# Two more slabs in the first wide stage of a four-branch decoder trunk, and its weights in 1 MB loads from one queue

## The chip, the cores and the metric

The kernel runs on one core of a Trainium2 chip. The metric is the device time in microseconds (us) of one execution; before the change it is 983.06 us, the median of three runs.

## The reference, cut to what matters

Two layers work on x, 256 tokens of 2048 numbers, all in float32. Each layer computes

```
c_act = silu(c)
shift, scl, gate_res = split(c_act @ ada_w[l] + ada_b[l], 3)   # 2048 x 6144 weights, one row of input
h = rms(x) * (1 + scl) + shift
z = h @ w_in[l]                      # layer 0: u_a, q, k, v, g = 48 slabs of 128 columns
y = [pool_mixer or attention ...]    # layer 0: pooling mixer of u_a beside attention of q, k, v
x = x + gate_res * ((y * silu(g)) @ w_out[l])                  # 16 slabs
```

So h of layer 0, which every product of that layer needs, waits for 32 MB of `ada_w`, and those weights serve one single row of input: they cost transfer time and VectorE time, but almost no TensorE time.

## The kernel before

**Weights as slabs.** `w_slabs` holds 141 slabs of 128 columns, 1 MB each, in the order of use: layer 0 has U (0 to 7), q (8 to 15), k (16 to 23), v (24 to 31), g (32 to 47) and its output product (48 to 63); layer 1 begins at 64. From slab 12 on, a slab is split into an upper and a lower part, `whi` (ScalarE, L496) and `wlo` (VectorE, L1204), and h likewise into `hhi` and `hlo`; TensorE makes three products of the fast kind for each of the 16 chunks of h (L835 to L837, for k and v L980 to L983). A slab goes through the buffer `raw` (four halves of 512 KB), loaded two slabs ahead (`AHEAD`).

**The first wide stage.** Slabs 0 to 11 are done differently. TensorE multiplies them unsplit (L893, `unsplit_chunk`): for each chunk c of h in turn it adds the chunk's product to all 12 outputs at once, which stand in six PSUM banks. So it can begin with chunk 0 when a quarter of the `ada_w` sums is there. The weights of this stage are stored chunk by chunk, and a half slab of `raw` is used up after 8 products. The trace has two records for one unsplit product and one for each fast one.

**Units and pieces.** `ada_w` comes as 192 units of 512 KB, 16 to a piece (1024 columns). Pieces 0 to 3 are layer 0's shift and scale: piece p gives chunks 4p to 4p+3 of h. VectorE multiplies each unit by its element of `c_act` and adds it to `acc` (L1214); the units of pieces 2 and 3 are done in two instructions each (L1231, L1234), so that the first half of a piece is ready after 8 units. TensorE sums `acc` over the partitions (L927, `reduce_piece` and `reduce_half`), VectorE keeps the result and normalizes x (L1238, L1251, L1287), and ScalarE adds the shift (L514). The first 64 units use eight slots: four in `ada`, two in `V`, two in `Y`; later ones use the four in `ada`. `UNIT_RATES` says how many units belong to the step of a slab; the units of pieces 4 to 11 are spread over all later stages.

**Order.** All orders are written out by hand, engine by engine, and tied by semaphores. SyncE (SP) issues the units and the slabs from 10 on; ScalarE issues slabs 0 to 9 between its own instructions, and waits there for TensorE to free the halves. SP's queue waits where its next transfer waits. On TensorE `keep_warm` puts small products without use ahead of some chunks (L822).

**Places further on that the change touches.** GpSimd clears `acc` for piece p+2 when piece p is summed (`clear`, L391), and in its program the slopes that the attention adds to the scores of heads 2 to 7 (`slopes`, L399) stand behind `clear(7)`, which waits for the sum of piece 5:

```
            slopes(0, range(0, 2))
            clear(7)
            slopes(0, range(2, HC))
```

Head i of layer 0 is scored on TensorE (L1005, L1006) at the end of step 27+i, and VectorE adds the slopes in the same step (L1387), takes the maxima, and divides (L1415) in the next; TensorE transposes the result (L1017). The weights of the pooling mixer, `PW`, are loaded into `V` by GpSimd (L432) before the first `pool_product` (L955), and `pool_branch` on VectorE makes its input. Where layer 1 begins, VectorE ends layer 0 with `add_x(63)` (L1343), and then makes the new h chunk by chunk with `lo` and `units` written between (L1599 to L1619); layer 1's wide stage (L874, 8 slabs, split) takes half slab c of slabs 64 to 71 for chunk c.

## Time and profile before

| | |
|---|---|
| runs, us | 979.67, 984.81, 983.06 |
| median | 983.06 us |
| span of the profiled execution | 977.3 us |
| device time of the profiled execution | not listed apart from the three runs; the lowest is 979.67 us |
| TensorE busy (PE) | 942.7 us, 96% of the span |
| VectorE busy (DVE) | 822.4 us, 84% |
| ScalarE busy (ACT) | 422.5 us, 43% |
| GpSimd busy (POOL) | 63.5 us, 6% |
| mean granted TensorE clock | 0.991 |
| HBM read over the span | 256.07 MB |

The span runs from the first instruction to the last. Matmuls are pipelined, so that a busy TensorE is not one at its peak: what counts is the distance from one matmul's start to the next. The granted clock is a share of 2.4 GHz; at 0.50 it is the lower level, 1.2 GHz.

### The profile page before, as it was taken

The page shows a single profiled execution, that of the slowest core. Times are in us where ns is not written, and L with a number is a line of the kernel's source. Part 1 is how long each engine was busy: PE and PEld are TensorE (multiplying, and loading weights), DVE is VectorE, ACT ScalarE, POOL GpSimd, SP SyncE. Part 2 cuts the span into 40 slices and gives each one's busy share as a digit, 9 for nine tenths or more (in the row PEclk, how much of TensorE's full clock was granted, in tenths as well). Part 3 has the DMA queues.
Part 4 walks back from the last instruction along what each step waited for, and adds up shares of the span by engine and source line. Part 5 has one row for each costly group of instructions (what it writes and reads, how often), then busy time and mean ns, then how long its engine had stood idle before and what let it go on. Part 6 is the DMA issues. An engine that isn't in the chain of part 4 may idle for free.

```text
span 977.3 us, 18750 instructions
## 1 busy us (share of the span) xinstructions
PE 942.7 (96%) x7042; PEld 908.3 (93%) x7042; DVE 822.4 (84%) x1256; ACT 422.5 (43%) x726; POOL 63.5 (6%) x76
## 2 busy tenths in 40 slices
PE   2999999999999999999999999999999999999998
PEld 2887889999998999999999999999999989998887
DVE  5887968887999778999887999888999986879964
ACT  2220125444655444444444444444556655743331
POOL 1000000010110000132100000000011100000000
PEclk9999998999999999999999999999999999999999
DMA  9999988888876878899959555544455445587962
GB/s 366 409 399 399 379 298 319 293 329 330 325 286 233 294 260 312 322 370 377 339 176 321 193 176 189 175 151 140 164 175 193 172 163 203 199 315 288 360 227 75
DMA packets 77666, 261.26 MB, mean 267 GB/s; under 512 B 7952, under 2 KB 8592, under 8 KB 77344
## 3 DMA queue, kind: packets, MB, share of 16 engines
q1 hardware_dynamic: 72384, 240.90, 67.5%
q10 hardware_dynamic: 2880, 10.49, 2.7%
q0 software_dynamic: 2336, 8.98, 2.6%
q8 instruction: 43, 0.70, 0.3%
q14 instruction: 23, 0.19, 0.1%
HBM read 256.07 MB, written 4.19 MB: 266 GB/s over the span
## 4 chain that ended last, share of the span: by engine, by line
PE 72%; DVE 19%; DMA 4%; issue 2%; ACT 2%; SPq 1%; DVEq 0%; ACTq 0%
PE bank L835 13%; PE bank L836 13%; PE bank L837 13%; PE bank L856 6%; DVE wlo L1204 5%; PE bank L893 4%; PE bank L980 4%; DVE acc L1214 4%; PE bank L983 4%; PE bank L982 4%; PE bank L854 3%; DMA Y<-ada_units 3%; DVE Y L1431 2%; PE bank L927 2%; DVE acc L1234 1%
## 5 line engine op out<-in xcount | busy, mean ns | idle before, releaser
L496 ACT ACTIVATE whi<-raw 128x1024 fp32r<-128x1024 f32 x256 | 270.1, 1060 | 382.3 <-PE bank L837 217.0
L1204 DVE TENSOR_TENSOR wlo<-raw,whi 128x1024 fp32r<-128x1024 f32 x256 | 312.0, 1234 | 74.9 <-ACT whi L496 73.6
L835 PE MATMUL bank<-hhi,whi 128*128 128x256 f32 x912 | 263.8, 289 | 2.5 <-ACT T L741 0.9
L836 PE MATMUL bank<-hlo,whi 128*128 128x256 f32 x912 | 259.3, 284 | 0.0
L837 PE MATMUL bank<-hhi,wlo 128*128 128x256 f32 x912 | 259.1, 284 | 0.0
L1214 DVE SCALAR_TENSOR_TENSOR acc<-ada,cact,acc 128x1024 f32<-128x1024 f32 x144 | 187.4, 1302 | 23.9 <-DMA ada<-ada_units 12.6
L835 PEld LDWEIGHTS bank<-hhi,whi 128*128 128x128 f32 x912 | 176.2, 193 | 5.3 <-issue 3.1
L836 PEld LDWEIGHTS bank<-hlo,whi 128*128 128x128 f32 x912 | 176.2, 193 | 0.1
L837 PEld LDWEIGHTS bank<-hhi,wlo 128*128 128x128 f32 x912 | 176.1, 193 | 0.0
L980 PE MATMUL bank<-whi,hhi 128*128 128x256 f32 x512 | 146.7, 287 | 0.0
L982 PE MATMUL bank<-whi,hlo 128*128 128x256 f32 x512 | 144.9, 283 | 0.0
L983 PE MATMUL bank<-wlo,hhi 128*128 128x256 f32 x512 | 144.9, 283 | 0.0
L980 PEld LDWEIGHTS bank<-whi,hhi 128*128 128x128 f32 x512 | 98.2, 192 | 0.8 <-issue 0.7
L1431 DVE SCALAR_TENSOR_TENSOR Y<-U,par,Y 128x256 f32<-128x256 f32 x240 | 98.6, 481 | 0.0
L982 PEld LDWEIGHTS bank<-whi,hlo 128*128 128x128 f32 x512 | 98.3, 192 | 0.1
L983 PEld LDWEIGHTS bank<-wlo,hhi 128*128 128x128 f32 x512 | 98.2, 192 | 0.0
L856 PE MATMUL bank<-both_g,whi 128*128 128x512 f32 x256 | 89.9, 399 | 0.0
L893 PE MATMUL bank<-X,raw 128*128 128x256 f32 x384 | 86.5, 387 | 1.6 <-DMA raw<-w_slabs 1.5
L893 PEld LDWEIGHTS bank<-X,raw 128*128 128x128 f32 x384 | 74.2, 195 | 12.2 <-issue 1.8
L835 PE MATMUL bank<-both_g,whi 128*128 128x256 f32 x256 | 73.1, 286 | 0.0
L836 PE MATMUL bank<-both_g,whi 128*128 128x256 f32 x256 | 72.5, 283 | 0.0
L837 PE MATMUL bank<-both_g,wlo 128*128 128x256 f32 x256 | 72.4, 283 | 0.0
(195 smaller groups left out, 1220.2 us busy)
## 6 DMA issues: line engine op xcount, KB each, us to landing
raw<-w_slabs SPq DMA_DIRECT2D x260, 512.0 KB, 4.5
ada<-ada_units SPq DMA_DIRECT2D x160, 512.0 KB, 6.6
raw<-w_slabs ACTq DMA_DIRECT2D x20, 512.0 KB, 7.0
V<-ada_units SPq DMA_DIRECT2D x16, 512.0 KB, 9.7
Y<-ada_units SPq DMA_DIRECT2D x16, 512.0 KB, 11.3
X<-xT SPq DMA_DIRECT2D x1, 2048.0 KB, 12.6
x_dram<-X POOLq DMA_DIRECT2D x4, 512.0 KB, 8.5
outT<-X POOLq DMA_DIRECT2D x3, 512.0 KB, 4.9
```

The source lines that it names most:

```text
L496: act.activation(whi[:, slot], raw[:, slot], ACT.Copy).then_inc(hi_done, 1)
L835: mm(out, whi[:, s, k, :], ahi[:, c, :], start=(c == 0), stop=False)
L836: mm(out, whi[:, s, k, :], alo[:, c, :], start=False, stop=False)
L837: last = mm(out, wlo[:, s, k, :], ahi[:, c, :], start=False, stop=(c == KC - 1))
L856: last = mm(out[:], whi[:, s, k, :], flat(both_g[:, c]), start=(c == 0), stop=(c == KC - 1), skip_group_check=True)
L893: last = mm(wide(s), raw[:, slot, k, :], X[:, c, :], start=(c == 0 and s % 2 == 0), stop=(c == KC - 1), skip_group_check=True)
L980: mm(out, hhi[:, c, tokens], upper, start=(c == 0 and q == 0), stop=False, skip_group_check=True)
L982: mm(out, hlo[:, c, tokens], upper, start=False, stop=False, skip_group_check=True)
L983: last = mm(out, hhi[:, c, tokens], lower, start=False, stop=(c == KC - 1), skip_group_check=True)
L1204: dve.tensor_tensor(wlo[:, s], source, whi[:, s].bitcast(F32), ALU.subtract)\
L1214: dve.scalar_tensor_tensor(acc[:, p % 2, :], unit_at(first + u), cact[:, bass.ds(k, 1)], acc[:, p % 2, :], ALU.mult, ALU.add).then_inc(ada ...
L1431: ins = dve.scalar_tensor_tensor(Y[:, j, :], U[:, j, k:k + SEQ], par[:, wcol:wcol + 1], Y[:, j, :], ALU.mult, ALU.add)
```

## The change

- `WIDE[0]` is 14: slabs 12 and 13 join the unsplit stage, in a seventh bank (`M`), and the split slabs begin with 14.
- The 14 slabs are loaded as 14 transfers of 1 MB (`load_wide`), all by SP, into four homes: the two pairs of halves of `raw`, `V` and `Y`. Slab i waits until TensorE has used up slab i-4. SP's one queue has them between the units: slab 0 after unit 15, then one after each four units, then slab 4 between units 31 and 32, and so on to slab 13 after unit 63.
- The first 64 units have twelve slots: four in `ada` and eight in `pre`, which shares its memory with `both_g`, not used yet.
- x is loaded in two parts of 1 MB behind units 0 and 1; before, it was one of 2 MB behind units 0 to 5.
- `keep_warm` goes from the wide stage; ten such products stand before it.
- The sums of pieces 4 to 7 are made in bank `XB`, not in `O`, and two pieces are summed later in the program: piece 4 after slab 22 (was 20), piece 5 ahead of slab 30 (was 28), piece 7 during slab 52 (was 50).
- `UNIT_RATES` begins with slab 12 (was 10), so the steps up to 33 take four units less and steps 62 to 65 one more each (two, not one).
- ScalarE evicts the 14 outputs in another order, with the split of slab 15 after the first two. `PW` is loaded after the last unsplit product, since `V` is now a home of slabs.

```
-UNIT_RATES = ((10, 34, 2), (34, 45, 1), (45, 47, 2), (47, 48, 1), (48, 62, 2),
-              (62, 70, 1), (70, 72, 2), ...
+UNIT_RATES = ((12, 34, 2), (34, 45, 1), (45, 47, 2), (47, 48, 1), (48, 66, 2),
+              (66, 70, 1), (70, 72, 2), ...
-WIDE = (12, 8)
+WIDE = (14, 8)
+RING = 12
+TILES = KC
+def wide_done(i):
+    return 2 * (i + 1) + 4
...
+        def load_wide(eng, i):
+            if i >= 4:
+                eng.wait_ge(pe_half, wide_done(i - 4))
+            eng.dma_start(wide_tiles(i), w_slabs[i:i + 1].rearrange("a p k n -> p (a k) n"))\
+               .then_inc(wide_in[i % 4], 16)
...
-            load_units(0, 6, None)
-            sp.dma_start(X[:], xT).then_inc(x_in, 16)
+            load_units(0, 2, None)
+            for part in range(2):
+                sp.dma_start(X[:, HC * part:HC * (part + 1), :], xT[:, HC * part:HC * (part + 1), :]).then_inc(x_in[part], 16)
...
+            load_units(2, UNITS - 2, None)
+            load_wide(sp, 0)
+            load_units(UNITS, 4, None)
+            load_wide(sp, 1)
...
+            for i, n in ((4, 0), (5, 3), (6, 6), (7, 9), (8, 13)):
+                load_wide(sp, i)
+                load_halves(2, n, {0: 3, 3: 6, 6: 9, 9: 13, 13: 16}[n])
+            for i, n in ((9, 0), (10, 4), (11, 8), (12, 12)):
+                load_wide(sp, i)
+                load_units(3 * UNITS + n, 4, None)
+            load_wide(sp, 13)
...
+            pool.wait_ge(pe_half, wide_done(UNSPLIT - 1))
             pool.dma_start(PW, pool_w).then_inc(pw_in, 16)
...
+            keep_warm(10, O[:, SEQ:SEQ + P])
...
-            for c in range(12):
+            for c in range(KC):
                 p = c // GROUP
                 if c % GROUP == 0 and p not in halved:
                     reduce_piece(p)
                     if p == 0:
                         spread_token(0)
-                    keep_warm(6, M)
...
-                if w == 20:
+                if w == 22:
                     reduce_piece(4)
             for w in range(V0, G0 + 5):
-                if w == V0 + 4:
+                if w == V0 + 6:
                     reduce_piece(5)
...
-            dve.wait_ge(acc_zero, 6)
-            run(dve, 18, 20, plain)
-            run(dve, 20, 22, plain)
-            keep_piece(4)
-            run(dve, 22, V0, plain)
+            for w in range(18, V0):
+                plain(w, None)
...
-                if w == V0 + 5:
+                if w == V0 + 1:
+                    keep_piece(4)
+                if w == V0 + 7:
                     keep_piece(5)
```

## Rows read from the trace of the kernel before

**Rows 1.** The page, part 4: shares of the chain that ended last.

```profile
PE 72%; DVE 19%; DMA 4%; issue 2%; ACT 2%; SPq 1%; DVEq 0%; ACTq 0%
```

**Rows 2.** Windows: stretch, length, busy us of PE, PEld, DVE, ACT, POOL, granted clock, DMA share, GB/s.

```profile
20.00:40.00 20.00, 19.18 (x89) 18.80 (x88) 16.24 (x25) 7.23 (x18) 0.95 (x1) 1.00 1.03 409
```

**Rows 3.** Timeline of PE in the first stage: start, length, line, operation, count, [idle before].

```profile
41.47 20.96 PE L893 MATMUL bank<-X,raw 128*128 128x256 f32 x96 [1.51 <-DMA raw<-w_slabs]
...
62.50 1.95 PE L927 MATMUL bank<-ones,acc 128*128 128x1 f32 x16
...
97.45 12.29 PE L893 MATMUL bank<-X,raw 128*128 128x256 f32 x48
...
127.24 0.95 PE L927 MATMUL bank<-ones,acc 128*128 128x1 f32 x8
...
129.70 10.63 PE L893 MATMUL bank<-X,raw 128*128 128x256 f32 x48
```

**Rows 4.** Timeline of ACT and DVE at the start.

```profile
17.64 0.72 ACT L508 ACTIVATE T<-X 128x256 f32<-128x256 f32 x2 [11.92 <-DMA X<-xT]
...
30.03 2.67 DVE L1214 SCALAR_TENSOR_TENSOR acc<-Y,cact,acc 128x1024 f32<-128x1024 f32 x2
```

**Rows 5.** Windows in the first stage.

```profile
100.00:102.00 2.00, 2.00 (x6) 1.59 (x5) 1.82 (x4) 0.75 (x2) 0.00 (x0) 0.50 1.01 401
```

**Rows 6.** Timeline of DVE: first instruction of three runs of seven units.

```profile
85.10 0.74 DVE L1231 SCALAR_TENSOR_TENSOR acc<-ada,cact,acc 128x512 f32<-128x512 f32 x1
...
99.26 0.75 DVE L1231 SCALAR_TENSOR_TENSOR acc<-ada,cact,acc 128x512 f32<-128x512 f32 x1
...
115.41 0.74 DVE L1231 SCALAR_TENSOR_TENSOR acc<-ada,cact,acc 128x512 f32<-128x512 f32 x1
```

**Rows 7.** The chain that ended last, slabs 13 to 15: start, length, what.

```profile
151.02 0.42 PE bank L835
159.41 0.34 PE bank L943 x4
...
165.94 1.83 PE bank L955 x8
173.53 0.34 PE bank L943 x4
```

**Rows 8.** DMA issues up to 160 us: count, KB each, us to landing.

```profile
V<-pool_w POOLq DMA_DIRECT2D x1, 1024.0 KB, 8.6
```

**Rows 9.** Timelines of PE, POOL and DVE in layer 0's attention.

```profile
251.41 1.84 PE L927 MATMUL bank<-ones,acc 128*128 128x1 f32 x16
...
267.94 0.38 PE L1028 MATMUL bank<-PTs,V 128*128 128x128 f32 x2
...
274.78 0.49 PE L1017 MATMUL bank<-ident,SP 128*128 128x128 f32 x3
...
254.23 1.36 POOL L399 TENSOR_SCALAR DS<-D 128x384 f32<-128x384 f32 x1
...
267.37 0.74 DVE L1387 SCALAR_TENSOR_TENSOR SP<-bank,rr,DS 128x128 f32<-128x128 f32 x2
...
273.79 0.55 DVE L1415 TENSOR_SCALAR SP<-SP,rl 128x128 f32<-128x128 f32 x2
```

**Rows 10.** Timelines of DVE, SP and PE where layer 1 begins.

```profile
476.01 1.27 DVE L1214 SCALAR_TENSOR_TENSOR acc<-ada,cact,acc 128x1024 f32<-128x1024 f32 x1
...
480.31 0.48 DVE L1343 SCALAR_TENSOR_TENSOR X<-bank,mod,V 128x256 f32<-128x256 f32 x1 [0.21 <-PE bank L837]
...
505.93 1.28 DVE L1214 SCALAR_TENSOR_TENSOR acc<-ada,cact,acc 128x1024 f32<-128x1024 f32 x1 [3.62 <-issue]
...
510.70 2.36 DVE L1204 TENSOR_TENSOR wlo<-raw,whi 128x1024 fp32r<-128x1024 f32 x2 [0.34 <-ACT whi L496]
...
499.24 0.43 SPq L317 DMA_DIRECT2D ada<-ada_units  x1
...
512.65 0.36 PE L874 MATMUL bank<-hhi,whi 128*128 128x256 f32 x1
```

More of the change, by code:

```diff
@@ L116, in build @@
         hlo = sb("hlo", [P, KC, SEQ], F32R)
+        with ExitStack() as early:
+            pre = early.enter_context(nc.sbuf_tensor("pre", [P, RING - 4, PIECE], F32))
         both_g = sb("both_g", [P, KC, 2, SEQ], F32R)
@@ L251, in half_uses @@
         def half_uses(w, half, t):
-            n = (2 * w + half) // 4 + 1
+            n = (2 * (w - UNSPLIT) + half) // 4 + 1
             return n if t is None else n + t
@@ L314, in load_units, with load_halves @@
                         sp.wait_ge(ada_done, unit + 1)
[L315 to L316 removed]
+                    elif unit >= RING:
+                        sp.wait_ge(ada_done, unit - RING + 5)
                     sp.dma_start(unit_at(n + u), ada_units[bass.ds(unit, 1)].rearrange("a p n -> p (a n)"))\
                       .then_inc(ada_in[unit_slot(n + u)], 16)
[L320 to L323 removed]
+            load_units(0, 2, None)
+            for part in range(2):
+                sp.dma_start(X[:, HC * part:HC * (part + 1), :], xT[:, HC * part:HC * (part + 1), :]).then_inc(x_in[part], 16)
+            def load_halves(p, first, last):
+                for n in range(first, last):
                     unit, half, u = UNITS * p + n, n // 8, n % 8
[L325 removed]
+                    sp.wait_ge(ada_done, unit - RING + 5)
                     sp.dma_start(unit_at(unit).rearrange("p (a n) -> p a n", a=2),
@@ L817, in _, with keep_warm @@
             mm = nc.tensor.matmul
-            def keep_warm(count, bank=PT):
+            def keep_warm(count, out=PT[:, 0:P]):
                 for _ in range(count):
-                    mm(bank[:, 0:P], ones[:], ident[:], start=True, stop=True)
+                    mm(out, ones[:], ident[:], start=True, stop=True)
             def slab(w, t, ahi, alo, gated_last=None, between=None):
@@ L888, in unsplit_chunk @@
                 for s in range(WIDE[0]):
-                    half, k = (WIDE[0] * c + s) // 8, (WIDE[0] * c + s) % 8
-                    slot = half_slot(0, half)
+                    i, k = (WIDE[0] * c + s) // TILES, (WIDE[0] * c + s) % TILES
                     if s == 0 or k == 0:
-                        pe.wait_ge(raw_in[slot], 16 * half_uses(0, half, None))
-                    last = mm(wide(s), raw[:, slot, k, :], X[:, c, :], start=(c == 0 and s % 2 == 0), stop=(c == KC - 1),
-                              skip_group_check=True)
-                    if k == 7:
+                        pe.wait_ge(wide_in[i % 4], 16 * (i // 4 + 1))
+                    last = mm(wide(s), wide_tiles(i)[:, k, :], X[:, c, :], start=(c == 0 and s % 2 == 0),
+                              stop=(c == KC - 1), skip_group_check=True)
+                    if k % 8 == 7:
                         last.then_inc(pe_half, 1)
@@ L924, in reduce_part @@
                         pe.wait_ge(mod_done, p)
-                    if p >= 6:
+                    if p >= 8:
                         pe.wait_ge(o_copied, HC if p < 10 else 2 * HC)
-                ins = mm(O[:, j:j + 1], acc[:, p % 2, j * P:(j + 1) * P], ones[:, 0:1], start=True, stop=True)
+                ins = mm(sums(p)[:, j:j + 1], acc[:, p % 2, j * P:(j + 1) * P], ones[:, 0:1], start=True, stop=True)
                 if j == HC - 1:
@@ L1067, in _ @@
                         spread_token(0)
-                    keep_warm(6, M)
                 if c % GROUP == GROUP - 1 and p + 1 in halved:
                     reduce_half(p + 1, 0)
-                if c % GROUP == 1 and p in halved:
-                    reduce_half(p, 1)
+                if c == 2 * GROUP + 1:
+                    reduce_half(2, 1)
+                if c == KC - 2:
+                    reduce_half(3, 1)
                 unsplit_chunk(c)
-            unsplit_chunk(12)
-            unsplit_chunk(13)
-            pe.wait_ge(ada_done, UNITS * 4 + 4)
-            for j in range(4, HC):
-                reduce_part(3, j)
-            keep_warm(6, M)
-            unsplit_chunk(14)
-            unsplit_chunk(15)
             def slab_stat(q0):
@@ L1124, in _ @@
             slab(48, None, ghi, glo, KC)
-            slab_g(49, None)
-            slab(50, None, ghi, glo, between=with_piece(7))
-            run(pe, 51, AB1, slab_g)
+            run(pe, 49, 51, slab_g)
+            slab_g(51, None)
+            slab(52, None, ghi, glo, between=with_piece(7))
+            run(pe, 53, AB1, slab_g)
             pe.wait_ge(stat_done, 2 * KC - 2)
```

153 lines of the change are left out of this document (65 added, 88 removed).

## The prediction

> **What bounds the kernel now.** I read the chain that ended last first: TensorE has 72% of it, VectorE 19%, transfers 4% [rows 1]. An average over the span hides stages, so I cut the start into windows next. Up to 116 us the transfers are full, at 409 GB/s [rows 2], and from 160 us on TensorE stands still almost nowhere. In between lies the first wide stage, and there the timeline shows three limits one after the other: transfers up to 62 us, then VectorE's units with TensorE waiting at 94, 110 and 128 us, then TensorE alone. It ends at 129.70 + 10.63 = 140.3 us [rows 3]. Two prices follow from the same views. An unsplit product is two records; 24 of them take 10.63 us, so one is 0.443 us, a chunk with 12 slabs is 5.3 us, a chunk with 14 is 6.2 us. A split slab, from 165.94 + 1.83 to 173.53, is 5.76 us [rows 7]. So an unsplit slab (16 x 0.443 = 7.1 us) is no cheaper on TensorE than a split one; it gains only where TensorE waits anyway.
>
> **The change part by part.**
>
> *Start of the wide stage.* x came after 5.46 MB (0.21 of parameters, six units, x) at 17.64 us; at 409 GB/s that is a lead of 4.3 us [rows 2, 4]. In the new order unit 2 is complete after 3.89 MB, at 13.8 us; VectorE then does 14 units at 1.39 us apiece (start to start) and ends piece 0 at about 33.2 us, where it ended at 30.03 + 2.67 = 32.7 [rows 4]. So the early x and the twelve slots gain nothing here: +0.5 us. Slab 0 (11.75 MB) is there at 33.0, so the 1.5 us for which TensorE waited for it at 41.47 [rows 3] go: chunk 0 at 40.0. Chunks 0 to 3 last 24.8 us, to 64.8.
>
> *Chunk 4.* The sum of piece 1 stands behind chunk 3: 64.8 + 1.95 = 66.8 [rows 3]. VectorE does unit 32 ahead of the normalization, and slab 4 now lies in front of it in the queue: 24.86 MB, 65.1 us, done at 66.7, so it does not set this. From a sum's end to the next chunk is 1.5 us (128.19 to 129.70, [rows 3]): chunk 4 at 68.3.
>
> *Clock.* After the gap at 94 to 96 us the granted clock fell to 0.50, the lower level, in 100 to 102 us [rows 5], and 24 products took 12.29 instead of 10.63 us [rows 3]: 1.7 us. Chunk 4 comes after such a gap, without the idle products that stood there. Nothing lost is the lower bound, 2.6 us (slab 13, 151.02 to 159.41 instead of 5.8 [rows 7]) the upper; I take 1.7, the nearest row. The Trainium skill, "TensorE: Matmul & The Clock Gate", Part 1, has this as a rule: an idle array is put to half its clock and sustained work lifts it, so taking `keep_warm` out speaks against the change. By it the last restart, at chunk 14, would cost as much again, and the sum below would be 1.7 us higher; by the row before chunk 14 it is nothing.
>
> *Chunks 4 to 15.* TensorE: chunks 4 to 6 and the half sum end at 68.3 + 1.7 + 18.6 + 0.95 = 89.6. VectorE's three runs of seven units begin 14.2 and 16.1 us apart (with the work between them) and last 11.4 us [rows 6]; the first begins 1.2 us after that half sum, at 90.8, the others at 105.0 and 121.1, and they end at 102.2, 116.4 and 132.5. TensorE is through chunk 8 at 102.0 and waits 0.2, through chunk 10 at 115.6 and waits 0.8; then chunks 11 to 13 run to 136.0, past the last unit. Sum and normalization 2.4, chunks 14 and 15 12.4: the stage ends at **150.9**, 10.6 us later. TensorE is now its limit. The transfers are ahead: slab 7, behind which units queue, is free to be issued at 73.5 us, and the full queue reaches it only at about 81.
>
> *To slab 16.* Before, slab 16 began at 173.53 + 0.34 = 173.9 [rows 7]. Now: 150.9, eviction 0.8, slab 14 5.8, to 157.5. Next is the first `pool_product`, and `PW`, formerly loaded at 129 us under cover, is issued at 150.9 and takes 8.6 us [rows 8]: 159.5, say 160 (lower bound: hidden, 157.5; upper: 162, with VectorE's split of slab 15 and pooling late too). Product 1.8, slab 15 5.8, statistics 0.3: 167.9. The clock after this gap costs 0 (as at 128 us) to 2.6 (as at 151 us); the gap lies between those, so I take half, 1.3: 169.2. **Term 1: -4.6 us** (11.5 for two split slabs and the old stall, against 10.6), from -8.5 to -0.5.
>
> *Head 2's slopes.* `clear(7)` is served by the sum of piece 5, now ahead of slab 30. VectorE adds head 2's slopes in step 29. From the start of that sum to the end of the slopes is 251.41 to 255.59, 4.2 us; the sum would begin when TensorE leaves head 0's product, at 268.3, so the slopes are there at 272.5, and VectorE's addition of 267.37 waits 5.1 us [rows 9]. Behind it in VectorE's queue stand the maxima, two units and a split, and the division, for which TensorE waits: it ended at 274.34, TensorE came at 274.78 [rows 9], so 0.4 us are absorbed. The 1.84 us of the sum are not extra, but taking them from slab 28 gives little, since VectorE paces those steps. **Term 2: +4.5 us**, from 2.5 (sum fully made good) to 5.1.
>
> *Entry of layer 1.* Four more units, 1.3 us each. That of step 62 stands before `add_x(63)`: VectorE's rows from 476.01 to 480.79 have no gap but 0.21 us [rows 10], so the normalization and chunk 0 are 1.1 us late. Those of steps 63 and 64 stand before the split of slab 66, which frees the buffer for slab 68 and the unit behind it in SP's queue; that unit was issued at 499.24, VectorE waited 3.62 us for it until 505.93, and the split of slab 68 followed (first half 511.9), 0.7 us ahead of chunk 8 at 512.65 [rows 10]. With 1.1 + 2.6 = 3.7 us on all of this, less the 0.7: **term 3: +3.0 us**, from 1.1 (only the first shows) to 4.3 (step 65's unit too). The units taken off slabs 12 and 13 went with those slabs' steps and give nothing here.
>
> *At no cost:* the sums' new bank and the later sums of pieces 4 and 7 (their results are used many slabs on; the same products in the same number); the order of evictions, under slab 14's 5.8 us, price 1 to 2 us if the statistics come late, inside the gap before `PW`; ScalarE's dropped issues, since it waited there for VectorE.
>
> **Sum:** -4.6 + 4.5 + 3.0 = +2.9 us, a span of 980.2. The profiled execution's own time is not listed; its span is 5.8 us below the median. Added to the median: **986.0 us**. What a measurement of this kernel can tell from no change is about 0.5%, 4.9 us.
>
> **Rivals.** *Faster, 975.5 us:* the two later waits hide (head 2's slopes, if the order on GpSimd is served sooner than I read; layer 1, if the unit transfers land sooner) and the clock stays up at both places: -4.6 - 1.3 - 1.7 = -7.6. For it: TensorE was 96% busy, with no wait over 1.5 us after 160 us. Against it: in both places the rows leave VectorE under a microsecond. *Slower, 991 us:* at layer 1's entry the delay isn't taken up by the 3.62 us in which VectorE waited for its unit, but lands behind it, since the unit is itself queued behind slab 68: 3.7 + 1.3 and a further 3 us for the queue behind two units where there was one, in place of 3.0; it decides once VectorE is over 5 us late at the split of slab 68. For it: 0.7 us of margin; against it: transfers are at only half load there. *Head of the queue, 995 us or more:* a slab load that waits for TensorE holds up units behind it, so VectorE starves and then TensorE. It decides when TensorE is over 7 us behind my times at chunk 4; beyond, it costs a microsecond for each. *No change at all in the wide stage's limit* (units still set it, end at 147): 982 us, within the middle case.
>
> **How the numbers follow.** Within 0.5%, my sum and its neighbours: 0.40, time 986, own range 980 to 988. Faster rival 0.27. Slower: 0.28 for the layer 1 rival and the upper bounds of terms 1 and 2 together, 0.05 for the queue. The low ends sum to -4.9, the high ends to +8.9 us; the range goes from the faster case's price, 975, to 993, and leaves out some 0.15.
>
> **What would show it.** Unsplit products ending at 149 to 153 us; chunk 4 at 67 to 69; no wait of TensorE for w_slabs; a gap before the first L955 of 1 to 4 us; slab 16 at 166 to 172. VectorE's third L1387 waiting 4 to 5 us for GpSimd, and TensorE's L1017 for L1415. L874 starting 1 us later relative to slab 48, and a stop at chunk 8. I am wrong if the stage ends below 147, if GpSimd's slopes are on time, or if units land late before 130 us.

## The result and the profile after

The changed kernel takes 984.67 us (median of 20 runs, 980.53 to 994.73), the kernel before 981.02 us (20 runs on the same chip, 976.79 to 984.81). The ratio, which is one of means, is 1.0053, with a 95% interval of 1.0034 to 1.0071: some 5 us slower (the means are 981.1 and 986.3 us). Predicted were 986.0 us, within 975 to 993, and +2.9 us against the profiled execution. The profiled execution of after has a span of 981.6 us, 4.3 us longer than before's 977.3.

The chain of waits of after reads (page, part 4; compare [rows 1]):

```profile
PE 46%; DVE 19%; DMA 3%; issue 3%; ACT 1%; SPq 0%; DVEq 0%; ACTq 0%
```

This view says little here: the shares listed add up to 72%, where before's came to 100%, so a good part of the chain was not put down to any engine. I therefore compared moments of the two timelines, in us from the start of each span:

| | before | after | gained or lost so far |
|---|---|---|---|
| last unsplit product ends | 140.3 | 150.3 | +10.0 (two slabs more) |
| slab 16 begins | 173.7 | 167.5 | -6.2 |
| first transpose of layer 0's attention | 259.8 | 252.9 | -6.9 |
| slab 48 begins | 386.2 | 385.4 | -0.8 |
| first product of layer 1's wide stage | 487.8 | 489.2 | +1.4 |
| its last product | 534.6 | 539.6 | +5.0 |
| span | 977.3 | 981.6 | +4.3 |

Unless the row says otherwise, the moments are starts in the timeline of PE or in the view of a line; they have slab 16 of before at 173.7 us, where the chain of [rows 7] gives 173.9. So the new first stage gives 6.2 us, the slabs up to attention 0.7 more, attention takes back 6.1, layer 1's entry 5.8 (2.2 up to its wide stage and 3.6 in it), and the rest of the kernel is 0.7 shorter. The rows of each follow.

*First stage.* Timeline of PE, start, length, line, operation, count and [idle before], to be read against [rows 3]:

```profile
33.91 3.58 PE L945 MATMUL bank<-ones,acc 128*128 128x1 f32 x16 [5.02 <-DVE acc L1224]
...
40.48 9.44 PE L911 MATMUL bank<-X,raw 128*128 128x256 f32 x32 [1.93 <-ACT X L532]
...
67.03 1.84 PE L945 MATMUL bank<-ones,acc 128*128 128x1 f32 x16
70.38 10.63 PE L911 MATMUL bank<-X,raw 128*128 128x256 f32 x48 [1.51 <-ACT X L532]
...
102.24 1.05 PE L945 MATMUL bank<-ones,acc 128*128 128x1 f32 x8 [0.48 <-DVE acc L1244]
...
116.40 1.05 PE L945 MATMUL bank<-ones,acc 128*128 128x1 f32 x8 [0.91 <-DVE acc L1244]
...
137.99 5.45 PE L911 MATMUL bank<-X,raw 128*128 128x256 f32 x24 [1.51 <-ACT X L532]
143.27 7.07 PE L911 MATMUL bank<-X,V 128*128 128x256 f32 x32
```

The stage ends at 143.27 + 7.07 = 150.3 us. TensorE never waits for w_slabs. The two half sums wait 0.48 and 0.91 us for VectorE's units. The first 32 records take 9.44 us where 32 take 7.07 further on: they ran at a lowered clock (0.74 granted over 40 to 50 us). A row ends where TensorE turns to a buffer of another name: the 48 behind 70.38 us are chunk 4 and most of chunk 5, the 24 at 137.99 most of chunk 14 (a chunk has 28). Below they are called by the chunk with which they begin.

*The step to slab 16*, same view:

```profile
156.99 0.95 PE L1106 MATMUL bank<-ones,QI 128*128 128x1 f32 x8
...
158.69 1.03 PE L1106 MATMUL bank<-ones,SG 128*128 128x1 f32 x8
159.58 1.97 PE L973 MATMUL bank<-Y,V 128*128 128x256 f32 x8
...
167.51 0.36 PE L998 MATMUL bank<-whi,hhi 128*128 128x256 f32 x1
```

`PW` was issued at 150.65 us and took 8.8 us (one row of POOL's issues), so it was there at 159.5; but from 157.0 to 159.6 TensorE was busy with 24 products of statistics behind slab 14. There is no gap to see, and no clock was lost behind it.

*Attention of layer 0.* DVE, POOL and PE, to be read against [rows 9]:

```profile
265.27 0.74 DVE L1397 SCALAR_TENSOR_TENSOR SP<-bank,rr,DS 128x128 f32<-128x128 f32 x2 [4.79 <-issue]
...
266.65 2.83 DVE L1224 SCALAR_TENSOR_TENSOR acc<-ada,cact,acc 128x1024 f32<-128x1024 f32 x2
269.40 2.35 DVE L1214 TENSOR_TENSOR wlo<-raw,whi 128x1024 fp32r<-128x1024 f32 x2
...
271.87 0.55 DVE L1425 TENSOR_SCALAR SP<-SP,rl 128x128 f32<-128x128 f32 x2
```

```profile
263.09 0.95 POOL L412 MEMSET acc<- 128x1024 f32 x1 [42.57 <-PE bank L945]
264.01 3.68 POOL L420 TENSOR_SCALAR DS<-D 128x384 f32<-128x384 f32 x3
```

```profile
261.18 1.84 PE L945 MATMUL bank<-ones,acc 128*128 128x1 f32 x16
```

The chain forecast under term 2 is there link by link: GpSimd waits 42.57 us for the sum of piece 5, which ends at 263.02; it clears; it makes the slopes; VectorE's addition has waited 4.79 us; behind it come the two units and the split, and only then the division, which ends at 272.4. The row of the addition names no releaser ("issue"). That it is the slopes follows from the times, since the first of the three instructions of 264.01 would be done near 265.3, where the addition begins, and from e1 below. TensorE's waits in this stretch (engine, line, releaser: us in total, times, longest) were 1.5 us in before, and in after

```profile
PE bank L1035 <- DVE SP L1425: 4.0, 4, 2.7
```

*Layer 1's entry.* TensorE's waits from 476 to 545 us, first before, then after:

```profile
PE bank L835 <- ACT T L741: 0.9, 1, 0.9
PE bank L835 <- DVE wlo L1204: 0.8, 1, 0.8
...
```

```profile
PE bank L893 <- DVE wlo L1214: 1.8, 2, 1.3
PE bank L924 <- ACT T L710: 1.3, 1, 1.3
PE bank L854 <- ACT T L760: 0.9, 1, 0.9
```

and DVE's and PE's timelines there, to be read against [rows 10]:

```profile
510.10 1.28 DVE L1224 SCALAR_TENSOR_TENSOR acc<-ada,cact,acc 128x1024 f32<-128x1024 f32 x1 [1.98 <-issue]
...
514.87 2.36 DVE L1214 TENSOR_TENSOR wlo<-raw,whi 128x1024 fp32r<-128x1024 f32 x2 [0.33 <-ACT whi L514]
```

```profile
502.28 0.36 PE L893 MATMUL bank<-hhi,whi 128*128 128x256 f32 x1 [1.31 <-DVE wlo L1214]
...
516.24 0.55 PE L893 MATMUL bank<-hhi,whi 128*128 128x256 f32 x1 [0.53 <-DVE wlo L1214]
...
516.81 0.41 PE L893 MATMUL bank<-hhi,whi 128*128 128x256 f32 x1
```

The longer of the two waits is the first: chunk 4's first product (502.28) waits 1.31 us for the split of slab 66, which VectorE begins at 500.91 us; in before it begins at 496.48. In front of it stand four units (5.45 us from 491.98) where before had two (2.67 us from 490.33). Chunk 8's first product (516.24) waits 0.53 us for the split of slab 68, and then the products last 0.41 us each where the split products at 151 us last 0.28: the clock has fallen behind the wait (510 to 520 us: 0.83 granted).

### The profile page after: what moved, and what is told of

Same layout as the page of the kernel before. It is cut to its first block, busy times and chain, and to the rows that moved or that the text cites. A ratio compares the mean times of both kernels' runs of the same rounds, so it can differ in the third digit from the quotient of the medians.

```text
span 981.6 us, 18557 instructions
## 1 busy us (share of the span) xinstructions
PE 943.0 (96%) x6994; PEld 906.2 (92%) x6994; DVE 818.3 (83%) x1252; ACT 418.2 (43%) x722; POOL 65.3 (7%) x76
## 4 chain that ended last, share of the span: by engine, by line
PE 46%; DVE 19%; DMA 3%; issue 3%; ACT 1%; SPq 0%; DVEq 0%; ACTq 0%
PE bank L854 11%; PE bank L855 10%; PE bank L856 10%; DVE wlo L1214 7%; DVE acc L1224 4%; DMA ada<-ada_units 3%; PE bank L875 3%; DVE Y L1441 2%; PE bank L873 2%; PE bank L998 1%; PE bank L1001 1%; PE bank L1000 1%; PE bank L893 1%; ACT whi L514 1%; PE bank L895 1%
## 5 line engine op out<-in xcount | busy, mean ns | idle before, releaser
L854 PE MATMUL bank<-hhi,whi 128*128 128x256 f32 x880 | 253.3, 288 | 1.7 <-ACT T L760 0.9
L855 PE MATMUL bank<-hlo,whi 128*128 128x256 f32 x880 | 248.9, 283 | 0.0
L856 PE MATMUL bank<-hhi,wlo 128*128 128x256 f32 x880 | 248.8, 283 | 0.0
L1224 DVE SCALAR_TENSOR_TENSOR acc<-ada,cact,acc 128x1024 f32<-128x1024 f32 x140 | 182.4, 1303 | 26.8 <-DMA ada<-ada_units 16.6
L854 PEld LDWEIGHTS bank<-hhi,whi 128*128 128x128 f32 x880 | 168.7, 192 | 4.5 <-issue 3.1
L855 PEld LDWEIGHTS bank<-hlo,whi 128*128 128x128 f32 x880 | 168.8, 192 | 0.1
L856 PEld LDWEIGHTS bank<-hhi,wlo 128*128 128x128 f32 x880 | 168.7, 192 | 0.0
L1000 PE MATMUL bank<-whi,hlo 128*128 128x256 f32 x512 | 145.5, 284 | 0.0
L856 PE MATMUL bank<-both_g,wlo 128*128 128x256 f32 x256 | 72.4, 283 | 0.0
L873 PE MATMUL bank<-both_g,wlo 128*128 128x256 f32 x240 | 68.1, 284 | 0.0
L875 PEld LDWEIGHTS bank<-both_g,whi 128*128 128x128 f32 x256 | 47.3, 188 | 10.7 <-DVE X L1350 0.5
```

Of the source, the lines that this page charges most:

```text
L854: mm(out, whi[:, s, k, :], ahi[:, c, :], start=(c == 0), stop=False)
L855: mm(out, whi[:, s, k, :], alo[:, c, :], start=False, stop=False)
L856: last = mm(out, wlo[:, s, k, :], ahi[:, c, :], start=False, stop=(c == KC - 1))
L873: mm(out[:, 0:SEQ], wlo[:, s, k, :], ghi[:, c, :], start=False, stop=False, skip_group_check=True)
L875: last = mm(out[:], whi[:, s, k, :], flat(both_g[:, c]), start=(c == 0), stop=(c == KC - 1), skip_group_check=True)
L1000: mm(out, hlo[:, c, tokens], upper, start=False, stop=False, skip_group_check=True)
```

## The experiments

All ratios are to the kernel before on the same chip. The edits are to the kernel after unless another base is named.

### e1: the slopes ahead of the clear

```
-            clear(7)
-            slopes(0, range(2, HC))
+            slopes(0, range(2, 5))
+            clear(7)
+            slopes(0, range(5, HC))
```

> The changed kernel with one move on GpSimd: the slopes of heads 2 to 4 are made before acc is cleared for piece 7, not after; nothing else. Theory A (head 2's slopes are late because they stand behind the clearing that the later sum of piece 5 serves): VectorE's third addition of slopes no longer waits, TensorE's waits for the division in layer 0's attention fall from 4.5 us to 1.5 to 2 us, the granted clock does not fall after them, and the time is 4 to 5 us under the changed kernel, a ratio to the kernel before of 1.000 to 1.002. Rival B (VectorE is simply full in these steps, and the sum of piece 5 costs the same wherever it stands): the waits stay within 1 us and the ratio is 1.004 to 1.006.

Measured: 1.0023 (1.0002 to 1.0044), mean 984.2 us. TensorE's waits for the division from 255 to 385 us fall back to before's size:

```profile
PE bank L1036 <- DVE SP L1426: 1.7, 4, 0.7
```

From the first transpose to slab 48 it takes 128.1 us; before took 126.4, after 132.5. Of the 6.1 us, 4.4 are back. What is left, 1.7 us, is about the sum of piece 5 itself (1.84 us), which now stands behind the transpose; no run takes it apart. The clock has a share too: e4, e6 and e7 below have after's order here and its wait of 2.7 us, but in their profiles the clock stays at 1.00 from 265 to 280 us, and the stretch takes 131.1 us. So 1.4 of the 6.1 us are the clock, and 4.7 the order.

### e2: four units drawn in attention, not at layer 1's entry

```
-UNIT_RATES = ((12, 34, 2), (34, 45, 1), (45, 47, 2), (47, 48, 1), (48, 66, 2),
-              (66, 70, 1), (70, 72, 2), ...
+UNIT_RATES = ((12, 34, 2), (34, 38, 1), (38, 42, 2), (42, 45, 1), (45, 47, 2), (47, 48, 1), (48, 62, 2),
+              (62, 70, 1), (70, 72, 2), ...
```

> The changed kernel with four units taken off steps 62 to 65 (one each again) and put on steps 38 to 41 (two each); nothing else. Theory A (the extra units at the entry of layer 1 delay VectorE, and through the order of its queue the split of slab 68): layer 1's wide stage starts 1 to 2 us earlier and has no wait for the split, from its first product to its last it takes 47 us as before the change and not 50, and the time is 4 to 5 us under the changed kernel, ratio 1.000 to 1.002. Rival B (those units fall into waits of VectorE for its own transfers and cost nothing; the loss there comes from TensorE being early or from the clock): the stage keeps its 50 us and the ratio is 1.004 to 1.006. Steps 38 to 41 have some 2 us of slack each on VectorE by the trace, so the move should cost nothing there.

Measured: 1.0012 (0.9989 to 1.0036), mean 982.2 us. The wait of L893 for `wlo` is gone, layer 1's wide stage takes 46.7 us instead of 50.4 (before: 46.8), and from slab 48 to its start it is 101.8 instead of 103.8 us (before: 101.6). In this profile that undoes term 3 completely.

### e3: both edits

> Both moves together on the changed kernel. Theory A (two separate waits, each on the path): the savings add up to 8 to 10 us, ratio 0.994 to 0.997, faster than the kernel before; what is left of the wide stage's gain (6.4 us at slab 16) then shows in the time. Rival B (VectorE paces steps 48 to 62 in any case, so what is won earlier is lost again before layer 1): no more than 5 us together, ratio 0.999 to 1.001.

Measured: 0.9961 (0.9942 to 0.9981), mean 978.6 us: faster than both kernels. With both late waits away, what is left of the change is term 1 and the 1.7 us in attention, and together they are worth 3.8 us.

### b1: the later sums alone, in the kernel before

```
-                if w == 20:
+                if w == 22:
                     reduce_piece(4)
...
-                if w == V0 + 4:
+                if w == V0 + 6:
                     reduce_piece(5)
...
-                    pe.wait_ge(mod_done, 6 if layer == 0 else 10)
+                    pe.wait_ge(mod_done, 4 if layer == 0 else 10)
...
-                if w == V0 + 5:
+                if w == V0 + 1:
+                    keep_piece(4)
+                if w == V0 + 7:
                     keep_piece(5)
```

> The kernel before with one part of the change alone: the sums of pieces 4 and 5 of the modulation taken two slabs later (at slabs 22 and 30 instead of 20 and 28) into their own bank, and attention's start asking for four pieces instead of six, so that the slopes of heads from the second on are made behind the first transpose as in after. Theory A (that part costs 4.5 us in attention, as after's profile shows with 4.5 us of waits for the division): +3 to +5 us, a ratio of 1.003 to 1.005, the stretch from the first transpose to slab 48 longer than 126.4 by 4 to 6 us, and the first stage and slab 16 as before. Theory B (the wait in after belongs to the other order of its vector work, not to the later sums): within 0.2%.

Measured: 1.0050 (1.0032 to 1.0068), +4.9 us: this part alone costs as much as the whole change. The stretch from the first transpose to slab 48 is 132.5 us as in after, VectorE's addition waits the same 4.79 us, and TensorE waits for the division:

```profile
PE bank L1017 <- DVE SP L1415: 5.0, 5, 2.7
```

### e4: one column a product in two slabs

```
+                    n = SEQ if s < 12 or c == 0 else 1
-                    last = mm(wide(s), wide_tiles(i)[:, k, :], X[:, c, :], ...
+                    last = mm(wide(s)[:, 0:n], wide_tiles(i)[:, k, :], X[:, c, 0:n], ...
```

> The changed kernel with the products of slabs 12 and 13 in the unsplit stage made over one token, not 256, from chunk 1 on; the loads, their order and all waits stay, and the two slabs' outputs are left out but for chunk 0. Theory A (TensorE's own products limit the stage with 14 slabs): it ends 7 to 9 us earlier, near 142 us, with VectorE's units as the limit again and TensorE waiting 1 to 4 us for the sums of pieces 2 and 3. Rival B (the 2 MB more of transfers or the queue's order limit it): it ends within 2 us of the changed kernel's 150.3 us.

The two slabs' outputs are made for one token only, so that this kernel leaves work out. Measured, one execution: 982.89 us, the stage's end at 151.0, no sooner. Timeline of PE:

```profile
137.90 7.13 PE L912 MATMUL bank<-X,raw 128*128 128x256 f32 x24 [1.51 <-ACT X L532]
144.88 6.13 PE L912 MATMUL bank<-X,V 128*128 128x1 f32 x32
```

The row's 32 are of both shapes; the groups of PE with the shapes apart (144 to 152 us; busy us, mean ns of one) have 8 narrow ones in them:

```profile
L912 PE MATMUL bank<-X,V 128*128 128x1 f32 x8 | 1.0, 229 | 0.0
```

The weight loads show their pace. Timeline of PEld from 144.87 to 145.5 us, where four narrow products and a wide one stand, and from 146.0 to 146.8, where all are wide:

```profile
144.88 0.64 PEld L912 LDWEIGHTS bank<-X,V 128*128 128x128 f32 x5
```

```profile
145.97 0.84 PEld L912 LDWEIGHTS bank<-X,V 128*128 128x128 f32 x4
```

A load lasts 0.19 us in both, so from one start to the next it is (0.64 - 0.19) / 4 = 0.11 us beside narrow products and (0.84 - 0.19) / 3 = 0.22 beside wide ones. The expectation of e7, written from this profile, reads 6.13 / 32 = 0.19 us as the pace of the loads; it is a mean of two paces that happens to equal a load's length. A narrow record costs half of a wide one. The Trainium skill, "TensorE: Matmul & The Clock Gate", Part 2, "Back-to-back issue gap", states that the spacing of products in a stream is set by load and product together; this trace agrees in that the product's columns change the spacing, and doesn't show what sets the 0.11 us that are left. The 60 narrow records of the stage are thus worth some 6 us, and yet nothing is gained, because the sums wait 3.3 us for VectorE's units (after: 1.4) and the clock falls at 70, at 117 and at 138 us.

### e7: those products left out

```
+                    if s >= 12 and 0 < c < KC - 1 and k % 8 != 7:
+                        continue
```

> The kernel after without most products of the thirteenth and fourteenth unsplit slabs: in contraction chunks 1 to 14 they are left out but for those on which a buffer's release hangs (24 products fewer), so the output isn't the reference's. All loads stay. The look with one column a product left the stage's end where it was, and its rows show why it could not tell: a 128 by 1 fp32 product took 229 ns against 380 to 407, but its weight load 190 to 200 ns all the same, so the engine's pace hardly moved (6.13 us for 32 of them, 7.07 for 32 full ones). Theory A (TensorE's weight loads pace the 14-slab stage): 24 products at 0.22 us are 5.3 us, and the stage ends at 145 to 146.5. Theory B (the weights' queue paces it): the products wait for tiles instead, and the end stays within 1.5 us of 150.4.

The expectation has two errors. It read the 32 of e4's timeline row as narrow ones, which the rows above correct, and it took an unsplit product for one record where it is two. Counted in the trace, 398 records of the product are left of 448: 50 fewer, 11.0 us at 0.221. That makes the result plainer. This kernel leaves out most of two slabs. Measured, one execution: the end at 149.8 us. Eleven microseconds of TensorE's work are away and 0.5 are gained. That is theory B's number but not its mechanism: TensorE waits for no weights, but for the sums, so for VectorE's units. Waits from 60 to 120 us, of PE and of DVE:

```profile
PE bank L947 <- DVE acc L1246: 5.8, 2, 4.0
```

```profile
DVE acc L1243 <- DMA pre<-ada_units: 3.5, 2, 2.4
DVE mod L1250 <- PE bank L947: 3.4, 1, 3.4
DVE acc L1243 <- DMA ada<-ada_units: 2.9, 2, 1.5
```

and PE's timeline behind the last of them:

```profile
114.84 1.87 PE L947 MATMUL bank<-ones,acc 128*128 128x1 f32 x8 [4.01 <-DVE acc L1246]
116.56 4.37 PE L913 MATMUL bank<-X,V 128*128 128x256 f32 x12
```

Up to that half sum 36 records are gone (8.0 us), and it begins 1.6 us sooner than in after. The sums wait 5.8 us instead of 1.4, VectorE waits 6.4 us for transfers instead of 2.3, chunk 4 begins 0.5 us later behind its sum and its clock costs 1.7. So there VectorE's units, with the transfers close behind, let TensorE be at most 1.6 us sooner. Behind it 14 records are gone (3.1 us), and the clock takes them: 0.8 us in the half sum, 1.5 in the 12 records after it (4.37 us against after's 2.84), 1.7 in chunk 14.

### e5: idle products ahead of chunk 0

```
                         spread_token(0)
+                        keep_warm(6)
```

> The kernel after with six idle products (bank PT, 128 columns) put back on TensorE right behind the first token spread, where the kernel before kept the engine busy ahead of its first chunk. The profile of after shows a granted clock of 0.57 and 0.74 at 30 to 50 us and its first 32 unsplit products at 9.44 us (0.295 us each, against 0.22 at full clock). Theory A (the half clock at the start is what the removed idle products cost): the first chunk runs at 0.22 each, chunk 4 (the first product behind the second set of sums) starts 1.5 to 3 us sooner than 70.4, and the stage's end moves from 150.4 to 147.5 to 149. Theory B (the stage's end is set by the weights' queue, which runs at about 400 GB/s from 30 to 150 us): the first chunk is faster, but the stage ends within 0.7 us of 150.4. Either way the whole kernel's time moves less than the stage's end, since slab 16 waits behind the statistics: A expects 0.997 to 0.999, B 1.000.

Measured: 1.0039 (1.0017 to 1.0060), after's result within its interval. Timeline of PE:

```profile
40.82 7.61 PE L911 MATMUL bank<-X,raw 128*128 128x256 f32 x32
...
69.48 12.16 PE L911 MATMUL bank<-X,raw 128*128 128x256 f32 x48 [2.11 <-ACT X L532]
```

Neither theory has the ratio. The stage's end is theory B's, but not for its reason: TensorE waits for no weights, and in after the transfers run at 175 to 300 GB/s from 120 to 150 us, not at 400. Chunk 0 is 1.8 us shorter and chunk 4 starts 0.9 us sooner, but in this execution chunk 4 runs at a lowered clock (12.16 instead of 10.63 us) and the stage ends at 151.0. Whether the first edit brings the second loss about isn't shown: after itself has the loss at chunk 4 in its second profile below.

### e6: x behind six units

```
-            load_units(0, 2, None)
+            load_units(0, 6, None)
...
-            load_units(2, UNITS - 2, None)
+            load_units(6, UNITS - 6, None)
```

> The kernel after with x behind six units again instead of behind two (still in two parts). Theory A (the prediction's: the early x gains nothing, since VectorE's units set the first sum): chunk 0 within 0.7 us of 40.5, slab 16 within 1 us of 167.5 where the clock is the same, a ratio within 0.002 of that of after (1.0053). Theory B (the early x pays for a part of the first stage, or six units ahead let VectorE run without its 5 us wait at unit 2): over 2 us either way, 1.003 or 1.0075.

Measured: 1.0062 (1.0038 to 1.0085), against after's 1.0053. Chunk 0 at 40.35 us (40.48), slab 16 at 167.6 (167.5). The early x gains nothing. This profile also tells what the slow chunk 0 isn't owed to. Timeline of PE, and the window of 40 to 50 us:

```profile
40.35 9.62 PE L911 MATMUL bank<-X,raw 128*128 128x256 f32 x32 [1.93 <-ACT X L532]
```

```profile
40.00:50.00 10.00, 9.64 (x33) 8.13 (x34) 9.37 (x10) 3.17 (x8) 0.00 (x0) 1.00 1.02 411
```

TensorE's idle products end here when the sum of piece 0 begins (34 us), so that the wait of 5.02 us is gone, and chunk 0's first 32 records take 9.62 us all the same. TensorE is slow there in before too: timeline of PE in before,

```profile
32.76 3.57 PE L927 MATMUL bank<-ones,acc 128*128 128x1 f32 x16 [0.78 <-DVE acc L1214]
```

3.57 us for a sum that takes 1.95 at 62.50 [rows 3]. In before 12 idle records follow (2.77 us) and chunk 0 is at full pace behind them. Over all profiles, the ten without idle products there lose 1.6 to 3.1 us on the first 32 records, and the four that have them lose 0 (before), 0.1 (e8), 0.5 (e5) and 1.8 us (b1). So the wait isn't the cause, and idle products help there more often than not. The window's granted clock of 1.00 contradicts the durations of its own records: at the start of a trace, go by how long equal products take.

### e8: all of it together

The edits of e1, e2, e5 and e6.

> The kernel after with all that the runs so far point to: slopes of three heads ahead of the last clear, the four unit pairs drawn earlier, six idle products behind the first token spread, and x behind six units instead of two. If the savings add up as the first three did (0.9961 with the first two): 0.993 to 0.996, slab 16 by 165 to 167 us, no wait of TensorE for the division over 1 us, and the wide stage of layer 1 at 46.7 us. A rival: the clock's stretches at half speed (0.66 and 0.83 in the profiles of e1 and e3) fall somewhere else and take the last two savings back: 0.996 to 0.998.

Measured: 0.9955 (0.9937 to 0.9973), mean 977.6 us, 974.6 to 981.1. It is the best version that does all of the work. In its profile slab 16 came at 172.0 us, not at 165 to 167, TensorE's longest wait for the division was 1.7 us, not under 1, and layer 1's wide stage took 48.6 us, not 46.7: of the expectation only the ratio held. The mean clock was 0.989 to 0.996 in all 12 runs. Its ratio is no better than e3's by what the intervals can tell, so the first two edits carry it.

### after and e3 once more

> The kernel after once more, for a second profile of it. Theory A (the stretches at half clock belong to the program's gaps): the first stage shows them at the same places, 0.57 and 0.74 at 30 to 50 us and none from 50 to 170, and the stage ends at 150.4 within 0.5 us. Theory B (which gap costs the clock differs between executions, as the profiles of the other versions suggest): a stretch at half clock in 70 to 80, 140 to 150 or 160 to 170 us in place of, or besides, the first, and an end later by 1.7 us for each.

> The kernel of e3 once more, for a second profile of it. Its first profile had a span of 982.9 us with 155.5 us for the stage's end and 0.66 to 0.83 of the clock in three stretches, though its timed runs are the fastest so far (978.7). Theory B (the lost clock was that execution's): the end at 150.5 to 152.5, and a span of 975 to 979. Theory A (it belongs to the kernel): the same 155.5, and the kernel would be faster still without it.

Measured: 990.72 and 975.25 us, spans of 988.9 and 973.4. Timeline of PE in the second profile of after:

```profile
67.37 1.84 PE L945 MATMUL bank<-ones,acc 128*128 128x1 f32 x16
70.73 13.49 PE L911 MATMUL bank<-X,raw 128*128 128x256 f32 x48 [1.51 <-ACT X L532]
...
141.20 7.13 PE L911 MATMUL bank<-X,raw 128*128 128x256 f32 x24 [1.51 <-ACT X L532]
```

and the windows of 70 to 80 us (length, busy us of PE, PEld, DVE, ACT, POOL, granted clock, DMA share, GB/s), first profile and second:

```profile
70.00:80.00 10.00, 9.62 (x45) 8.48 (x46) 9.27 (x15) 3.19 (x8) 0.00 (x0) 1.00 1.05 400
```

```profile
70.00:80.00 10.00, 9.27 (x30) 7.71 (x31) 8.93 (x15) 3.37 (x8) 0.23 (x1) 0.67 1.05 396
```

The same program, the same wait of 1.51 us, and chunk 4 takes 10.63 us once and 13.49 us once; at chunk 14 it is 5.45 and 7.13, at the first `pool_product` 1.97 and 2.98. The stage ends at 155.2 instead of 150.3 and slab 16 begins at 174.0: no sooner than before's 173.7, so the whole of term 1 is gone in such an execution. The 20 timed runs fall in two groups with nothing between them: 12 with spans of 978.7 to 983.7 us and a mean clock of 0.986 to 0.995, 8 with 987.3 to 992.9 us and 0.979 to 0.984. Their means are 7.2 us apart, and the two profiles 7.3. That the eight are those that lose the clock at chunk 4 rests on this likeness; only one of them has a profile. And the hole may be chance: the 12 runs of e6, the same program but for x, go from 981.5 to 990.1 us with no gap wider than 2.3 us, where after's is 3.6.

### e9: idle products ahead of chunk 4

On e3:

```
                         spread_token(0)
+                    else:
+                        keep_warm(6)
```

> The kernel of e3 with six idle products (bank PT, 128 columns) on TensorE between the sum of piece 1 and chunk 4, where the kernel before had them. Two profiles of after differ in one place: at 70 to 80 us the granted clock is 1.00 in one and 0.67 in the other, and the latter's stage ends at 155.3 us instead of 150.4, its span is 7.3 us longer. Of 20 timed runs of after twelve have spans of 978.7 to 983.7 us and a mean clock of 0.986 to 0.995, eight have 987.3 to 992.9 and 0.979 to 0.984. Theory A (the idle array of 1.5 to 2 us ahead of chunk 4 costs the clock in a part of the executions, and the idle products removed there were what kept it): granted clock at 70 to 80 us 1.00, no run's mean clock below 0.986, the highest time at least 3 us below e3's 984.7, and a ratio of 0.993 to 0.9955. Theory B (the clock falls whatever TensorE does there): the spread of e3's clock, 0.982 to 0.996, and a ratio of 0.995 to 0.998.

In this kernel the bank `PT` also holds the sum of slab 8 at that time, so the idle products write over part of that slab's sum; all other work is done. Measured: 0.9953 (0.9933 to 0.9974), mean 976.9 us. The highest of 12 runs is 980.6 us (e3: 984.7), the mean clock 0.986 to 0.996 (e3: 0.982 to 0.996). Timeline of PE:

```profile
68.24 1.58 PE L842 MATMUL bank<-ident,ones 128*128 128x128 f32 x12
69.89 10.63 PE L912 MATMUL bank<-X,raw 128*128 128x256 f32 x48
...
137.50 7.07 PE L912 MATMUL bank<-X,raw 128*128 128x256 f32 x24 [1.51 <-ACT X L533]
```

Chunk 4 is at full clock and theory A holds in all its numbers. Chunk 14, whose idle products were also removed by the change and were not put back here, lost 1.6 us in this execution. The mean is 1.7 us below e3's, which the intervals alone don't separate; the shorter tail is what supports it, and one profile at full clock is no proof, since after has one too without idle products. Idle products in a free bank at both places were not tried.

Nor do idle products always hold the clock. The profile of before, timeline of PE and the window of 64 to 66 us:

```profile
64.31 2.77 PE L822 MATMUL bank<-ident,ones 128*128 128x128 f32 x12
...
128.05 1.58 PE L822 MATMUL bank<-ident,ones 128*128 128x128 f32 x12
```

```profile
64.00:66.00 2.00, 2.00 (x13) 2.00 (x13) 1.93 (x6) 0.54 (x2) 0.95 (x1) 0.62 1.04 389
```

Ahead of chunk 4 the clock fell although the 12 idle records stood there (1.58 us at full clock, 2.77 here). But most of the slow stretch fell on products that nobody needs: from the start of the sum (62.50) to chunk 4 (66.88) it took 4.4 us, where after takes 3.4 (67.03 to 70.38), and the chunk's 72 records took 16.21 us instead of the 15.79 that 72 take from 111.62 us. So before paid some 1.5 us there in that execution, and after in its second profile 2.9.

## Why the prediction was right, and where its steps were not

*The number.* The forecast change of +2.9 us measured +4.3 in spans and +5.1 in means. That 986.0 lies 1.3 us from the measured median is better than the sum deserves, since it was added to a median of three runs (983.06) that is 2.0 above that of twenty. All three terms came out larger than forecast: 1.6 us more gain in the first, 1.6 and 2.8 us more loss in the others. The second (6.1 against at most 5.1) and the third (5.8 against at most 4.3) lie outside their own bounds in this profile; the sum holds because the first has the other sign, which is luck.

*Term 1 (-4.6): right in kind; it measured -6.2 in the profiled execution.* The end of the stage came at 150.3 against 150.9, and the sums waited where and about as long as forecast (0.5 and 0.9 against 0.2 and 0.8 us). But two errors of 2 us cancel in it. Chunk 4 began at 70.4, not 68.3: 0.5 us because chunk 0 was put at 40.0 without the +0.5 just worked out (it began at 40.48), the rest because chunk 0 ran at a lowered clock, a place at which I had charged no clock at all; and chunk 4, which I charged 1.7 us, lost nothing. The remaining difference at slab 16 is the 1.3 us of clock behind the first `pool_product`, not paid, and 0.4 us of its start. That start is right by accident: I had it wait for `PW` at 160, and had left out the 2.6 us of statistics that fill the time.

*The clock: the step that was mis-sized.* I took one price (1.7 at chunk 4, half of 2.6 later) as if an execution paid it. The two profiles of after show nothing in one and 2.9 us at chunk 4, 1.7 at chunk 14 and 1.0 at the `pool_product` in the other; over all versions each place loses or not by itself. By the profiles' granted clock and the timed runs, 12 of 20 executions cost on average 983.4 us, 2.3 above before's mean of 981.1, close to the forecast sum of +2.9; the other 8 took 990.6, or +9.4. The mean of both is the measured +5.1. Before had idle products ahead of chunks 0, 4 and 14, and its mean clock never was below 0.986 in the runs of these comparisons, though they didn't hold the clock at every place and time (e6 and e9 above). That the missing idle products are the cause is supported by e9 for chunk 4, by a difference that the intervals don't settle, and only argued for chunk 14. The Trainium skill, "TensorE: Matmul & The Clock Gate", Part 1, states that an idle array falls to half its clock and that the point at which the clock changes isn't tied to the kernel's start and varies from run to run. The traces agree: the same 1.5 us wait costs nothing in one execution and 2.9 us in the next. By its rule chunk 14 would cost 1.7 us too, and I had dropped that for a single row of before; the second profile of after shows it. That row was no evidence either: before had 12 idle records in that very gap (128.05 us), and the change takes them out.

*Term 2 (+4.5): right in its chain.* The addition waited 4.8 us (forecast 5.1), and b1 gives +4.9 us (3.1 to 6.7) for this part alone. In the profile it is 6.1 us, and 4.7 where the clock stays up (e4, e6, e7). TensorE's own longest wait was 2.7 us, not 4.7; the 1.84 us of the sum, which I had called not extra, and the lowered clock behind the wait (0.83 at 270 to 280 us) make up most of the rest. e1 took back 2.9 us by the ratios and 4.4 by the trace.

*Term 3 (+3.0): right place, too small, and the larger stop overlooked.* The unit of 505.93 ran at 510.10, 4.2 us later (forecast 3.7), and slab 68's split followed it at 514.87; the stop at chunk 8, on which I had put the term, came to 0.53 us. I had the two units in front of slab 66's split delay only what comes after it, and didn't ask when TensorE needs that split itself: chunk 4 waits 1.31 us for it, and 0.9 to 1.7 us in all six other profiles with these units, while chunk 8 waits in only three of the six. The table puts 5.8 us on this stretch: 2.2 up to the stage, where I had 1.1, and 3.6 in it, of which 1.8 are the two waits and most of the rest is the clock behind the second. Up to the stage it is even 3.9 to 4.3 us in five of the six other profiles; where those microseconds go is open. e2 took back 4.0 us by the ratios. I had priced a wait by its length and not by what TensorE's clock does behind it.

*TensorE as the stage's limit: wrong in the form in which I wrote it.* With 11.0 us of its work away the stage ends 0.5 us sooner (e7). Up to 116 us VectorE's units let TensorE be no more than 1.6 us sooner; from there on TensorE is alone, but behind the waits that a lighter load opens it lost what was left to the clock in this one execution. The end was right since both limits had been worked out and lay together.

*At no cost:* the early x: right (e6 without it is 0.9 us slower than after, well inside the intervals). The twelve slots were not tested by themselves.

*Rivals.* The faster one needed both waits hidden and was ruled out by the rows of both. The one on layer 1's queue fell: the unit landed 1.98 us late for VectorE instead of 3.62, so the delay was partly taken up. The queue's head never held TensorE up. Eight executions of twenty came near 991 (990.6 on average), for another reason than either rival gave.

The two fixes give 2.9 and 4.0 us alone and 9.0 together; each ratio has an interval of 2 us either way, so whether they do more than add up is open.

## What to carry to other kernels

A stage that saves 6 us on the engine that bounds the kernel can be given back whole by two small moves that seem free: a sum put later, for which another engine's clear waits with needed work queued behind it, and vector instructions put in front of one for which TensorE waits. Look for what is queued behind each moved instruction, and undo each part by itself: here that turned +0.5% into -0.4%. Where idle products in front of a known stop are taken out, one profile doesn't price it; look at the spread of the runs and at the mean clock of each, since the loss may fall on a part of the executions only.

## What the runs showed of the hardware

- One wait of 1.51 us in front of the same products left the granted clock at 1.00 in one execution of a program and at 0.67 over the next 10 us in another (10.63 and 13.49 us for the 48 records of 24 unsplit products).
- The place at which it falls is no property of the kernel: chunk 4's 48 records took 10.63 us in four profiles (after, e6, e3 again, e9), 12.2 to 12.3 in two (e5, e2) and 13.45 to 13.49 in four (after again, e1, e3, e8), where one record of e3's is missing and e8 had waited 3.05 us; chunk 14's 24 took 5.45 or 7.1 us, and not always as chunk 4 did (e9: 10.63 and 7.07, e5: 12.16 and 5.45).
- Twelve idle records of 128 columns in front of a stream took 1.58 us at full clock and 2.77 at the lowered one. With them the clock fell at 64 to 68 us in the profile of before and stayed up there in those of b1 and e9.
- The listed clock can miss a slow stretch at the start: e6 has 1.00 from 30 to 50 us, and 32 records there took 9.62 us against 7.07 later.
- A record of an fp32 product over one column took 229 ns and one over 256 columns 382 ns, and both had a weight load of 190 ns. But the loads overlap: one starts 0.11 us after the other beside narrow products and 0.22 us beside wide ones (e4). The length of a record is not the pace of a stream.
